# Down projections split by token half and column half; the next stage's first tiles begin on tokens 0 to 127 while the other half is normed; eight weight buffers in places; all steps placed anew

## The chip, the cores and the metric

One core of a Trainium2 chip runs the kernel. The time is device microseconds of one execution; the kernel before has a median of 1056.41 us over three runs (1062.69, 1056.41, 1053.89). One more execution was profiled. PE is TensorE (PEld its weight loads), DVE is VectorE, ACT is ScalarE, POOL is GpSimd, SP is SyncE.

## What is computed

Two transformer blocks on 256 tokens of width 1024, in fp32 (16 meta tokens are put ahead in the first block). Cut to the skeleton:

```
# first block
u = rms_norm(h, mix_pre_g);  proj = u @ w_in
y_a = hgrn2_mixer(...) @ w_hg_o;  y_b = mla_mixer(...) @ w_mla_o
h = h + rms_norm((gate_a * y_a + gate_b * y_b) @ w_out, mix_post_g)       # stage out1
u = rms_norm(h, ffn_pre_g)                                                # x2
h = h + rms_norm((silu(gt) * up) @ w_ffn_out, ffn_post_g)                 # stage ffn1, 22 tiles of 128
# second block
h = rms_norm(x, attn_pre_norm)                                            # x3
o_moba, o_nsa, o_diff, o_swa = four attentions on h @ w_in_2              # stage maps
x = x + rms_norm(mix @ w_out_2, attn_post_norm)                           # stage out2
h = rms_norm(x, ffn_pre_norm)                                             # x4
x = x + rms_norm((gelu(conv(h @ w_gate)) * (h @ w_up)) @ w_down, ffn_post_norm)   # stage ffn2, 32 tiles
```

A down projection here is any of the four products that write the 1024 columns of all tokens and are followed by a norm over those columns: out1, ffn1, out2, ffn2. The norm after it, the residual, and the next stage's own norm must be finished for a token before any matmul of the next stage can use that token.

## The kernel before

**Products.** Every large product is done with fp32r operands in two parts: a weight w is split into `wh` (rounded) and `wl = w - wh`, an activation into R parts h and l, and `three` issues three matmuls: wh with h, wh with l, wl with h. A projection tile (`gemm`) has the weights as the loaded operand and 256 tokens moving, 8 blocks x 3 = 24 matmuls of 256 columns, into one PSUM bank. A step `down` has the activations as the loaded operand and the weights moving: for a block k of 128 rows it does two token halves c (tokens 0 to 127, then 128 to 255) and in each two column halves h, 2 x 2 x 3 = 12 matmuls of 512 columns, into four banks.

**Weights.** They come in slabs of two units (a unit is 128 x 1024); three slab buffers `raw`, loaded by SP in order. A unit is made by a step `split`: ACT (or DVE) rounds it into `wh`, then DVE or POOL subtracts it into `wl`. There are four unit buffers (`NUNIT = 4`), and unit u goes into buffer u % 4, so its split waits until unit u - 4 is used. `POOL_UNITS` lists the units whose `wl` is POOL's.

**Order.** `schedule` writes one list of steps; every engine walks the whole list and does its own part of each step, strictly in this order. Where jobs are woven between projection tiles, a string of `MIX` says which comes next ("." a main step, a letter a step of that job). The list is written out by hand or by search, nothing decides at run time.

**Around a norm.** `tail` does the last blocks of a down projection (four for the 8-block ones, three for ffn1 and ffn2), first all of c = 0, then all of c = 1. Then for each c: `post` (ACT squares two column halves, DVE multiplies by the gain, then sum, variance, square root, reciprocal), `res` (DVE adds into X, two halves of 512 columns), `norm` (ACT squares X, variance, square root, reciprocal, ACT and DVE scale half of X each). Then `turn` transposes both token halves on PE, and eight steps `pre` make the h part (ACT, 256 columns) and the l part (DVE) of the next stage's operand x2, x3 or x4. Only then the next stage's first `gemm` can start. `maps` lets POOL make 12 bias tiles and lets it load two buffers `w1`, for the compression jobs `cmp_hid`.

Of the kernel before, what the change touches and what calls it, by code (L numbers as in the profile page):

```python
# [12 lines left out]
D = 1024  # L13
NM = 16
T1 = 272
HID1 = 22
HID2 = 32
LAG = 3
# [3 lines left out]
NUNIT = 4  # L22
# [116 lines left out]
class Plan:  # L139


    def __init__(self):
        self.blocks, self.at, self.slots = [], {}, []
        self.lo = lambda u: "dve"
# [7 lines left out]

    def slot(self, step, blocks, *behind):

        done = self.weights(step, blocks)
        out = [step, *behind] + [("split", u + NUNIT, self.lo(u + NUNIT), "act") for u in done]
        self.slots.append(out)
# [39 lines left out]
def down_tail(plan, name, order, order_out, mix):  # L197


    w, _, kt = DOWN[name]  # L200
    ks = order[kt - (4 if kt == 8 else LAG):]
    units = [u + NUNIT for u in plan.weights(("tail", name), [(w, 128 * k, rng(128 * j)) for k in ks for j in range(8)])]
    chain = [(kind, name, c) for c in range(2) for kind in ("post", "res", "norm")]
    order_out.append(("tail", name))
    for c in mix:
        order_out.append(chain.pop(0) if c == "." else ("split", units.pop(0)) + MAKERS[c])
    assert not chain and not units


def schedule(mixes, pool_units):  # L210
    p = Plan()
    p.lo = lambda u: "pool" if u in pool_units else "dve"
    order = [("start",)] + [("split", u, "pool" if u == 0 else "dve", "dve" if u == 0 else "act") for u in range(1)]
    order += [("turn", "x1")] + [("pre", "x1", k) for k in range(8)]
    order += [("split", u, "dve", "act") for u in range(1, NUNIT)]
    order += [("bounds",)]

    for n in range(8):
        p.tile("hf", n)
# [6 lines left out]
    order += flat(p.take())  # L226
# [24 lines left out]
    order += weave(p.take(), [metas, scan(0), scan(1), *lats, read(0) + read(1)], mixes["scan"])  # L251
# [16 lines left out]
    order += weave(p.take(), [[("o_norm",)] + [("o_scale", h) for h in range(0, 8, 2)]] + heads, mixes["latent"])  # L268

    for n in range(8):  # L270
        p.tile("yb", n)
    order += flat(p.take()) 
    for k in range(4):
        p.wide(("down", "out1", k), "w_out", k, [rng(128 * j) for j in range(8)])
    order += flat(p.take())
    down_tail(p, "out1", list(range(8)), order, mixes["out1"])

    def ffn(name, gate, up, x, nt):
        order.append(("turn", x))
        order.extend(("pre", x, k) for k in range(8))  # L280
        for i in range(nt):
# [5 lines left out]
        order.extend(flat(p.take()))  # L287
        down_tail(p, name, list(range(nt)), order, mixes[name])

    ffn("ffn1", "g1", "u1", "x2", HID1)  # L290

    order += [("maps",), ("turn", "x3")] + [("pre", "x3", k) for k in range(8)]
    o, w = IN2, "w_in_2"
    p.tile("nkc", 0, True)
    for n in range(2):
        p.tile("nq", n, True)
# [3 lines left out]
    for k in range(8):  # L300
        p.wide(("tm1", k), w, k, [rng(c) for c in (o["mv"], o["mv"] + 128, o["dv"], o["dv"] + 128)],
               *([("tm1_out",)] if k == 7 else []))
    for n in (0, 2, 1, 3):
        p.tile("d", n, True)
# [22 lines left out]
    order += weave(p.take(), jobs, mixes["maps"])  # L327
    down_tail(p, "out2", KORD2, order, mixes["out2"])
    ffn("ffn2", "g2", "u2", "x4", HID2)
    order.append(("store",))  # L330
    last = -(-len(p.blocks) // 16) * 2
    return [s for s in order if s[0] != "split" or s[1] < last], p.blocks, p.at
# [1714 lines left out]
```

## Time and profile before

| | us |
|---|---|
| three runs | 1062.69, 1056.41, 1053.89 |
| median | 1056.41 |
| profiled execution | 1064.89 |
| its span, first to last instruction | 1063.1 |
| PE busy in the span | 989.7 |
| DVE, ACT, POOL busy | 519.4, 480.3, 357.9 |
| mean granted clock of PE, 1 is full | 0.958 |

A PE that is busy is not PE at its peak: at the lower of its two clock levels it is busy for twice as long with the same matmuls. So two things are to be looked for: where PE is idle, and where its clock is low. The profiled execution took 8.5 us more than the median of the runs.

### The profile page before, as it was taken

Reading aid. Unit: us, or ns where it says so; the run is one execution under the profiler, and the core shown is the slowest. Engines: PE = TensorE matmul, PEld = TensorE weight load, DVE = VectorE, ACT = ScalarE, POOL = GpSimd, SP = SyncE. Lnnn points to the kernel's source line nnn. Section 1 sums busy time; section 2 is a strip of 40 time slices with the busy share of each in tenths; the row PEclk is TensorE's granted clock in tenths of the full one; section 3 lists DMA queues with packets and bytes.
Section 4 is the critical chain, followed back from the end, with each engine's and each line's share of the span. In section 5 each row is a group of like instructions: output and inputs, shape, how many; then the busy total and the mean of one; then the engine's idle time right before and its main releaser. Section 6 shows DMA issues by size and latency. Waiting matters only on the chain.

```text
span 1063.1 us, 16460 instructions
## 1 busy us (share of the span) xinstructions
PE 989.7 (93%) x6733; PEld 900.4 (85%) x6733; DVE 519.4 (49%) x1027; ACT 480.3 (45%) x843; POOL 357.9 (34%) x167
## 2 busy tenths in 40 slices
PE   3999999979999988999999498999979999999997
PEld 3989999967788968999999396887769999999996
DVE  5414855256424764423433625575365455465455
ACT  5424113454335355444444625366454444444443
POOL 1322221211023435244333542120064633534551
PEclk9999969999999998999999698899889999999999
DMA  7434222333133344555545343222335555554551
GB/s 270 168 131 159 80 80 104 111 123 119 40 120 140 138 158 178 176 186 186 199 166 198 118 159 105 75 90 80 119 108 190 198 174 184 199 188 173 194 174 65
DMA packets 23035, 154.80 MB, mean 146 GB/s; under 512 B 2592, under 2 KB 3104, under 8 KB 5168
## 3 DMA queue, kind: packets, MB, share of 16 engines
q1 hardware_dynamic: 22384, 151.65, 39.8%
q0 software_dynamic: 576, 2.10, 0.6%
q8 instruction: 54, 0.88, 0.3%
q14 instruction: 21, 0.17, 0.0%
HBM read 152.42 MB, written 1.05 MB: 144 GB/s over the span
## 4 chain that ended last, share of the span: by engine, by line
PE 83%; DVE 8%; ACT 5%; DMA 2%; issue 1%; SPq 0%; POOL 0%; DVEq 0%; ACTq 0%; POOLq 0%
PE pb L433 82%; ACT FA L439 3%; PE pb L436 2%; DVE FA L442 2%; DMA FA<-in_lev 1%; DVE st L442 1%; DVE wl L442 1%; DVE X L448 1%; DVE R L448 1%; ACT wh L439 1%; DVE st L445 1%; ACT R L439 1%; DMA FA<-in_w 0%; DVE FA L448 0%; SPq L469 0%
## 5 line engine op out<-in xcount | busy, mean ns | idle before, releaser
L433 PE MATMUL pb<-R,wh 128*128 128x256 f32 (+1 forms) x3056 | 570.2, 288 | 11.5 <-POOL wl L442 7.2
L442 POOL TENSOR_TENSOR wl<-raw,wh 128x1024 fp32r<-128x1024 f32 x140 | 340.5, 2438 | 654.1 <-ACT wh L439 652.0
L433 PEld LDWEIGHTS pb<-R,wh 128*128 128x128 f32 x3056 | 487.3, 194 | 22.2 <-issue 11.6
L433 PE MATMUL pb<-R,wl 128*128 128x256 f32 (+1 forms) x1528 | 437.3, 286 | 0.0
L439 ACT ACTIVATE wh<-raw 128x1024 fp32r<-128x1024 f32 x273 | 286.1, 1054 | 183.8 <-PE pb L433 183.7
L433 PEld LDWEIGHTS pb<-R,wl 128*128 128x128 f32 x1528 | 296.8, 194 | 0.0
L442 DVE TENSOR_TENSOR wl<-raw,wh 128x1024 fp32r<-128x1024 f32 x138 | 182.1, 1323 | 209.3 <-ACT wh L439 209.0
L433 PE MATMUL pb<-wh,R 128*128 128x512 f32 (+1 forms) x744 | 242.9, 393 | 1.6 <-DVE FA L457 1.0
L433 PEld LDWEIGHTS pb<-wh,R 128*128 128x128 f32 x744 | 141.2, 190 | 32.1 <-issue 2.3
L433 PE MATMUL pb<-wl,R 128*128 128x512 f32 (+1 forms) x372 | 145.2, 390 | 0.0
L439 ACT ACTIVATE FA<-pb 128x256 f32<-128x256 f32 (+7 forms) x155 | 65.7, 436 | 166.1 <-PE pb L433 147.2
L433 PE MATMUL pb<-FA 128*128 128x64 f32 (+14 forms) x696 | 111.8, 310 | 4.1 <-ACT FA L439 2.1
L433 PEld LDWEIGHTS pb<-FA 128*128 128x128 f32 (+6 forms) x696 | 88.9, 199 | 21.3 <-issue 9.9
L433 PEld LDWEIGHTS pb<-wl,R 128*128 128x128 f32 x372 | 71.1, 191 | 12.0
L436 PE MATMUL pb<-cst,FA 128*128 128x128 f32 (+4 forms) x213 | 40.4, 329 | 43.6 <-ACT FA L439 34.9
L442 DVE TENSOR_TENSOR FA<-FA,pb 128x256 f32<-128x256 f32 (+2 forms) x64 | 28.0, 437 | 94.2 <-PE pb L433 86.0
L436 PEld LDWEIGHTS pb<-cst,FA 128*128 128x128 f32 (+4 forms) x213 | 28.5, 163 | 53.4 <-ACT FA L439 31.3
L439 ACT ACTIVATE R<-FA 128x256 fp32r<-128x256 f32 (+1 forms) x66 | 28.4, 431 | 94.1 <-DVE FA L442 94.1
L442 DVE TENSOR_TENSOR R<-FA,R 128x256 fp32r<-128x256 f32 (+1 forms) x58 | 28.7, 495 | 29.0 <-ACT R L439 29.0
L439 ACT ACTIVATE FA<-FA 128x256 f32<-128x256 f32 (+7 forms) x39 | 16.0, 410 | 53.3 <-DVE FA L448 47.2
L442 DVE TENSOR_TENSOR FA<-FA 128x512 f32<-128x512 f32 (+7 forms) x68 | 38.1, 602 | 3.7 <-PE pb L433 1.8
L448 DVE SCALAR_TENSOR_TENSOR FA<-pb,sm,FA 128x255 f32<-128x255 f32 (+1 forms) x68 | 33.9, 498 | 10.4 <-ACT FA L439 8.0
(95 smaller groups left out, 408.6 us busy)
## 6 DMA issues: line engine op xcount, KB each, us to landing
raw<-in_w SPq DMA_DIRECT2D x139, 1024.0 KB, 4.8
X<-in_x SPq DMA_DIRECT2D x2, 512.0 KB, 4.4
post<-in_ffn_post SPq DMA_DIRECT2D x2, 512.0 KB, 5.6
post<-in_w POOLq DMA_DIRECT2D x2, 512.0 KB, 4.8
FA<-in_w POOLq DMA_DIRECT2D x2, 512.0 KB, 4.6
out<-X SPq DMA_DIRECT2D x4, 256.0 KB, 2.0
cst<-in_cst SPq DMA_DIRECT2D x1, 796.0 KB, 12.5
post<-in_mix_post SPq DMA_DIRECT2D x1, 512.0 KB, 3.6
```

The lines of the kernel that those rows point to most:

```text
L433: return self.real.matmul(*a, **k) if self.real else self
L436: return self.real.transpose(*a, **k) if self.real else self
L439: return self.real.activation(*a, **k) if self.real else self
L442: return self.real.tensor_tensor(*a, **k) if self.real else self
L445: return self.real.tensor_scalar(*a, **k) if self.real else self
L448: return self.real.scalar_tensor_tensor(*a, **k) if self.real else self
```

## The change

Four things are changed together.

- **Tails.** `tail` is now four steps (c, h), each all of its last four blocks for one token half and one column half, 12 matmuls of 512 columns. The last four blocks are taken everywhere (`LAG` is 4). `post` waits for each column half by itself. A partial variance is made from the first half, and one ACT instruction adds the second half and takes the root; this takes one DVE instruction out of each of the two norms.
- **Next stage by token halves.** `chain` does post, res, norm, then `turn` and two steps `op` of four blocks for one token half, then the same for the other. For x2 and x4 the first two tiles of gate and up are split: `gemm0` does the 8 matmuls of `wh` with both parts of tokens 0 to 127 (256 columns in two pieces of 128), `gemm1` later the 16 others. Their result lies in two halves of the bank, and DVE folds them (`tensor_reduce`). For x3 the value projections `tm2` and `tm1` are brought to the front, all of c = 0, then all of c = 1.
- **Buffers.** From out1's tail to the last block of x3's value projections, and again in ffn2, there are eight unit buffers; PLACE and PRIOR give each unit its buffer and the unit that it replaces. Four of them lie where upper parts of `FA` are at other times, so the first units in them wait for these (`opened`).
- **All steps placed anew.** All strings of MIX are new, and `MADE` gives every unit its makers: ACT rounds 219 units (273 before) and DVE 59 (5), DVE subtracts 176 (138) and POOL 102 (140). `maps` is moved behind the value projections; the jobs of the attentions start only after it.

The diff, cut to its core:

```
-LAG = 3
+LAG = 4
-NUNIT = 4
+NBASE = 4
+NWIDE = 8
+SPLIT_TILES = 2
...
+def chain(name, x):
+    out = []
+    for c in range(2):
+        out += [("post", name, c), ("res", name, c)]
+        if x:
+            out += [("norm", name, c), ("turn", x, c), ("op", x, c, 0), ("op", x, c, 1)]
+    return out
...
+        return [[("tail", name, c, h)] for c in range(2) for h in range(2)], units
...
+        for i in range(SPLIT_TILES):
+            for t in (gate, up):
...
+                main.append([("gemm0", t, i)])
+        main += [[("gemm1",) + s[0][1:3]] + s[1:] for s in late]
+        segs.append((down, main, [chain(down, x), refill(units, list(range(first, first + NWIDE - NBASE)))]))
...
+    main += [[s[0] + (0,)] for s in both] + [[s[0] + (1,)] + s[1:] for s in both]
+    segs.append(("ffn1", main, [chain("ffn1", "x3"), refill(units, [])]))
+    wide[0] = wide[0][0], p.next_unit()
+    fixed(("maps",))
...
-    "out1": ".p....p.pq",
+    "out1": "...............bbaaab.abaa.aaba...aaab.bb...",
...
+                elif kind == "gemm0":
...
+                        e.matmul(both, whi(u, o), OPERAND[src][:, k, :, 0:128], start=k == 0, stop=False)
+                elif kind == "gemm1":
...
+                        e.matmul(both, whi(u, o), OPERAND[src][:, k, :, 128:256], start=False, stop=False)
+                        m = e.matmul(b[:, 0:256], wlo(u, o), operand(src, k, 0), start=False, stop=k == 7)
...
+                elif kind == "op":
+                    x, c, i = a
+                    for j in range(4):
+                        k = 4 * i + j
+                        e.wait_ge(*pe.at(("turn", x, c, j)))
+                        if i:
+                            e.wait_ge(*dve.at((x, "l", j, c)))
+                        e.activation(operand(x, k, 0)[:, 128 * c:128 * c + 128], banks.of(("turn", x, c, j))[:, 128 * i:128 * i + 128],
+                                     ACT.Identity, scale=sc(PRE_GAIN[x], k)).then_inc(*act.up((x, "h", k, c)))
```

PE behind out1's last down matmuls, before: the 16 transposes of both token halves (`cst,FA`), then the first gate tile.

```order
1393 L433 MATMUL pb<-wh,R 128x512
1394 L436 MATMUL pb<-cst,FA 128x128 x16
1395 L433 MATMUL pb<-R,wh 128x256 x2
1396 L433 MATMUL pb<-R,wl 128x256
1397 L433 MATMUL pb<-R,wh 128x256 x2
```

and now:

```order
1390 L484 MATMUL pb<-wh,R 128x512
1391 L487 MATMUL pb<-cst,FA 128x128 x8
1392 L484 MATMUL pb<-R,wh 128x2x128 x32
1393 L487 MATMUL pb<-cst,FA 128x128 x8
1394 L484 MATMUL pb<-R,wh 128x2x128
1395 L484 MATMUL pb<-R,wl 128x256
```

The transposes are halved, and 32 matmuls (four `gemm0`) stand between the halves; the other 64 matmuls of these four tiles follow behind the second half (the first two rows of them are shown).

ACT in the same place, before, from the table load for the square root on (`wh<-raw` are splits, `FA,st<-pb` the squares of post, `FA,st<-X` those of norm, `R<-pb,sm` the operand):

```order
196 L439 ACT_TABLE_LOAD
197 L439 ACTIVATE st<-st 128x1
198 L439 ACTIVATE FA,st<-pb 128x512 x2
199 L439 ACTIVATE st<-st 128x1
200 L439 ACTIVATE wh<-raw 128x1024
201 L439 ACTIVATE FA,st<-X 128x512 x2
202 L439 ACTIVATE st<-st 128x1
203 L439 ACTIVATE FA<-X,st 128x512
204 L439 ACTIVATE FA,st<-pb 128x512 x2
205 L439 ACTIVATE st<-st 128x1
206 L439 ACTIVATE wh<-raw 128x1024
207 L439 ACTIVATE FA,st<-X 128x512 x2
```

and now:

```order
180 L490 ACTIVATE FA,st<-pb 128x512 x2
181 L490 ACTIVATE st<-st 128x1
182 L490 ACTIVATE FA,st<-X 128x512 x2
183 L490 ACTIVATE st<-st 128x1
184 L490 ACTIVATE FA<-X,st 128x512
185 L490 ACTIVATE wh<-raw 128x1024
186 L490 ACTIVATE R<-pb,sm 128x128 x8
187 L490 ACTIVATE FA,st<-pb 128x512 x2
188 L490 ACTIVATE st<-st 128x1
189 L490 ACTIVATE wh<-raw 128x1024
190 L490 ACTIVATE FA,st<-X 128x512 x2
191 L490 ACTIVATE st<-st 128x1
```

The eight operand instructions of c = 0 and a split now stand ahead of the first square of c = 1.

DVE in the same place, now (`FA<-pb,post` is the gain, `X<-FA,st,X` res, `R<-pb,sm,R` the l part of the operand):

```order
326 L496 TENSOR_SCALAR FA<-X,st 128x512
327 L508 CAST wh<-raw 128x1024
328 L493 TENSOR_TENSOR wl<-raw,wh 128x1024
329 L499 SCALAR_TENSOR_TENSOR R<-pb,sm,R 128x128 x8
330 L496 TENSOR_SCALAR st<-st 128x1
331 L493 TENSOR_TENSOR FA<-pb,post 128x512 x2
332 L511 RECIPROCAL st<-st 128x1
333 L499 SCALAR_TENSOR_TENSOR X<-FA,st,X 128x512 x2
334 L493 TENSOR_TENSOR wl<-raw,wh 128x1024
335 L496 TENSOR_SCALAR st<-st 128x1
336 L511 RECIPROCAL st<-st 128x1
```

A whole split of DVE stands between the scaling of X and the operand of c = 0, and a subtraction inside the norm of c = 1; before, DVE had no subtraction there.

PE behind ffn1's last down matmuls, now (before, 16 transposes and then a gate-like tile, as above):

```order
2291 L484 MATMUL pb<-wh,R 128x512
2292 L487 MATMUL pb<-cst,FA 128x128 x8
2293 L484 MATMUL pb<-wh,R 128x268
2294 L484 MATMUL pb<-wl,R 128x268
...
2325 L484 MATMUL pb<-wl,R 128x512
2326 L484 MATMUL pb<-wh,R 128x512
2327 L487 MATMUL pb<-cst,FA 128x128 x8
2328 L484 MATMUL pb<-wh,R 128x268
```

Between the transposes of the two halves stand 24 matmuls of 268 and 24 of 512 columns.

## Rows read from the trace of the kernel before

**Rows 1.** The page, part 2: busy tenths in 40 slices, and the granted clock.

```profile
PE   3999999979999988999999498999979999999997
PEclk9999969999999998999999698899889999999999
```

**Rows 2.** Busy time in windows, PE: window, busy (matmuls), clock, DMA share, GB/s.

```profile
392.00:408.00 16.00, 8.46 (x43) 0.68 0.27 99
592.00:616.00 24.00, 9.43 (x44) 0.57 0.24 88
772.00:788.00 16.00, 8.68 (x49) 0.68 0.28 98
140.00:162.00 22.00, 22.00 (x112) 0.53 0.14 48
```

**Rows 3.** The timeline behind out1's tail: start, length, engine, operation.

```profile
388.06 0.60 ACT L439 ACTIVATE FA<-pb 128x512 f32<-128x512 f32 x1 [2.86 <-PE pb L433]
...
390.39 1.42 DVE L448 SCALAR_TENSOR_TENSOR X<-FA,st,X 128x512 f32<-128x512 f32 x2
...
391.19 2.87 POOL L442 TENSOR_TENSOR wl<-raw,wh 128x1024 fp32r<-128x1024 f32 x1 [5.04 <-ACT wh L439]
...
392.60 1.47 DVE L442 TENSOR_TENSOR st<-st 128x1 f32<-128x1 f32 x1 [0.79 <-ACT FA L439]
...
393.07 0.39 PE L433 MATMUL pb<-wh,R 128*128 128x512 f32 x1
...
394.73 0.72 ACT L439 ACTIVATE FA<-X,st 128x512 f32<-128x512 f32 x1 [0.23 <-DVE st L460]
...
403.33 3.00 ACT L439 ACTIVATE R<-pb,sm 128x256 fp32r<-128x256 f32 x8
...
403.81 3.23 DVE L448 SCALAR_TENSOR_TENSOR R<-pb,sm,R 128x256 fp32r<-128x256 f32 x8 [0.97 <-ACT R L439]
404.35 0.79 PE L433 MATMUL pb<-R,wh 128*128 128x256 f32 x2
...
407.08 0.41 PE L433 MATMUL pb<-R,wh 128*128 128x256 f32 x2
...
407.44 0.40 PE L433 MATMUL pb<-R,wh 128*128 128x256 f32 x2
```

**Rows 4.** The timeline behind ffn1's tail.

```profile
591.83 5.32 POOL L442 TENSOR_TENSOR wl<-raw,wh 128x1024 fp32r<-128x1024 f32 x2 [3.61 <-ACT wh L439]
592.10 5.60 DVE L448 SCALAR_TENSOR_TENSOR X<-FA,st,X 128x512 f32<-128x512 f32 x2
...
592.36 0.39 PE L433 MATMUL pb<-wh,R 128*128 128x512 f32 x1
...
611.46 0.79 PE L433 MATMUL pb<-R,wh 128*128 128x256 f32 x2 [2.39 <-DVE R L448]
```

**Rows 5.** The timeline behind out2's tail.

```profile
772.76 0.39 PE L433 MATMUL pb<-wh,R 128*128 128x512 f32 x1
...
783.83 0.78 PE L433 MATMUL pb<-R,wh 128*128 128x256 f32 x2
```

**Rows 6.** Busy time in the window of maps: PE, PEld, DVE, ACT, POOL, clock, DMA, GB/s.

```profile
611.50:762.20 150.70, 140.23 (x906) 119.96 (x907) 75.42 (x279) 73.95 (x199) 34.47 (x26) 0.92 0.29 101
```

**Rows 7.** Groups by shape: count, busy us, mean ns of one, idle before.

```profile
L439 ACT ACT_TABLE_LOAD x16 | 20.5, 1283 | 1.0 <-PEq L2037 0.7
...
L439 ACT ACTIVATE FA<-FA,st 128x256 f32<-128x256 f32 x24 | 11.9, 496 | 0.0
...
L439 ACT ACTIVATE FA<-FA,st 128x128 f32<-128x128 f32 x24 | 9.5, 395 | 11.7 <-DVE st L445 11.7
...
L442 DVE TENSOR_TENSOR wl<-raw,wh 128x1024 fp32r<-128x1024 f32 x138 | 182.1, 1323 | 209.3 <-ACT wh L439 209.0
...
L457 DVE CAST wh<-raw 128x1024 fp32r<-128x1024 f32 x5 | 3.3, 686 | 0.5 <-PE pb L433 0.5
...
L448 DVE SCALAR_TENSOR_TENSOR FA<-FA,st 128x128 f32<-128x128 f32 x4 | 1.4, 342 | 0.0
```

More of the change, by code:

```diff
@@ L286, in ffn @@
                 p.wide(("down", name, i - LAG), DOWN[name][0], i - LAG, [rng(128 * j) for j in range(8)])
[L287 to L292, printed above, removed]
+        segs.append((None, p.take(), []))
+        return first
+    for n in range(8):
+        p.tile("yb", n)
+    for k in range(4):
+        p.wide(("down", "out1", k), "w_out", k, [rng(128 * j) for j in range(8)])
+    wide = [(ffn("ffn1", "g1", "u1", "x2", HID1, "out1", list(range(8)), p.take()), 0)]
     o, w = IN2, "w_in_2"
-    p.tile("nkc", 0, True)
-    for n in range(2):
-        p.tile("nq", n, True)
+    main, units = down_tail("ffn1", list(range(HID1)))
     for k in range(8):
@@ L326, in schedule @@
             jobs.append(plain((m, h)) + ([("join", kt + h // 2)] if h % 2 else []))
[L327 to L332, printed above, removed]
-KORD2 = [2, 3, 4, 5, 6, 7, 0, 1]
-POOL_UNITS = (5, 8, 9, 10, 14, 15, 16, 24, 25, 27, 28, 30, 31, 32, 34, 38, 39, 40, 42, 44, 47, 50, 52, 54, 60, 61, 63,
[5 rows of a table removed]
+    segs.append(("maps", p.take(), jobs))
@@ new lines, in segments @@
+    wide.append((ffn("ffn2", "g2", "u2", "x4", HID2, "out2", KORD2, []), 10 ** 6))
+    tail, units = down_tail("ffn2", list(range(HID2)))
+    segs.append(("ffn2", tail, [chain("ffn2", None)]))
+    fixed(("store",))
+    count = -(-len(p.blocks) // 16) * 2
+    last, place, prior, after = {b: -NWIDE + b for b in range(NWIDE)}, [], [], {}
+    for u in range(count):
+        n = NWIDE if any(a <= u < b for a, b in wide) else NBASE
+        b = min(range(n), key=lambda b: (last[b], b)) if u >= NBASE else u
+        place.append(b)
+        prior.append(last[b] if last[b] >= 0 else None)
+        if last[b] >= 0 and u not in early:
+            after.setdefault(last[b], []).append(u)
+        last[b] = u
@@ new lines, in named, with names @@
+    def named(s):
+        if s[0] == "free":
+            return [("split", u) for u in after.get(s[1], []) if s[1] not in behind]
+        if s[0] == "open":
+            return [("split", s[1])]
+        if s[0] == "behind":
+            return [("split", u) for u in after.get(s[1], [])]
+        return [s]
+    def names(steps):
+        return [t for s in steps for t in named(s)]
+    segs = [(key, [names(s) for s in main], [names(j) for j in jobs]) for key, main, jobs in segs]
+    return segs, p.blocks, p.at, place, prior, [a for a, _ in wide], wide[0][1]
@@ L728, in bank, with down @@
                 return b
-            def down(name, k, c, first, last):
+            def down(name, k, c, first, last, hs=(0, 1)):
                 src = DOWN[name][1]
```

389 lines of the change are left out of this document (226 added, 163 removed), and 5 rows, old and new, of the table POOL_UNITS.

## Prediction

> **What bounds the kernel now.** I read the slices first [rows 1]: PE is at nine tenths or full nearly everywhere, with a hole at the start, three marked holes in the middle (slices 15 and 16, 23, 30) and one at the end. So PE bounds, and only what fills a hole or keeps the clock up shortens the run. The middle holes are the norms behind out1, ffn1 and out2. The windows over them [rows 2] show PE busy for 8.46 of 16 us, 9.43 of 24 and 8.68 of 16, at a clock of 0.68, 0.57 and 0.68: at the lower of the two levels (1.2 of 2.4 GHz) for much of it. The timeline gives the size of each hole. The last tail matmul starts at 393.07 and lasts 0.39; the next stage's first matmul starts at 404.35 [rows 3]: 10.9 us. The 12 matmuls up to 407.08 take 2.73 us, where at full clock three take 0.36 (407.08 to 407.44), so 12 take 1.44: another 1.3 us. Behind ffn1: 592.75 to 611.46 [rows 4], 18.7 us; its clock is at the lower level to about 615.3 (estimated from the 0.57 over 24 us, which leaves 3.4 us at full clock in the window), so half of 3.8 us, 1.8 with rounding, is lost beside it, 20.5. Behind out2: 773.15 to 783.83 [rows 5], 10.7 us, and 1.0 at low clock (estimated from the 0.68 in the same way), 11.7. Sum: 12.2 + 20.5 + 11.7 = 44.4 us.
>
> Two more losses are in no hole: the clock is 0.53 over 22 us from 140 on though PE is always busy (10.3 us lost), and maps, 150.7 us long, has 10.5 us of idle PE and a clock of 0.92 (12 us) [rows 6].
>
> **A chain for one token half.** Let 0 be the end of its last tail matmul. Before, c = 0 begins at 388.06 and ACT has scaled X at 394.73 + 0.72, 7.4 us later [rows 3]. In this stand 1.3 us in which a DVE instruction of one column takes 1.47 instead of 0.15 beside POOL's subtraction that started at 391.19. Behind ffn1 it is worse: two residual additions take 5.60 beside two subtractions of POOL, against 1.42 behind out1 [rows 3, 4]. Now: the square of the first column half lies under the tail, the second takes 0.8 with its accumulator, the root and reciprocal 0.9, the residual 1.4 (rows 3: 1.42 for two), the second square of X 0.8 behind it, root and reciprocal 0.55, scaling 0.72: **5.2 us**, if POOL isn't in the way. Then the transposes (about 0.1 each, one pair is enough to begin) and `op`. An `op` instruction on 128 columns is in no row for its operands: 256 columns cost ACT 3.00 / 8 = 0.375 and DVE 0.40 apiece [rows 3], 128 cost DVE 0.34 in another form [rows 7]. I take 0.30 for a pair in step, near that row, with ends 0.20 (half of the 256-column price) and 0.40 (all of it).
>
> **out1.** PE has 24 matmuls of c = 1 to do in the meantime: 388.0 to 393.46, 5.45 us [rows 3]. ACT has a split (1.05) behind the scaling and begins `op` at 6.3. DVE has a cast and a subtraction, 0.69 + 1.25 ([rows 7]: 0.686, and 1.323 as a mean with the waits beside POOL), from 5.0 to 7.0. So the first `gemm0` matmul starts at 7.3, 1.85 after PE went idle. Its eight blocks come at 0.30 each, not at 0.12, so this tile ends at 9.5 instead of 8.3: 1.3. The other three tiles run at 0.12 x 24 = 2.9, to 12.4. The second half does not start at 5.45, since its squares stand in ACT's list behind the eight operand instructions (order of the section on the change): ACT is free at 8.6. From there two squares and their accumulators 1.6, root and reciprocal 0.9 (the gain of DVE lies between), residual 1.4, then DVE's subtraction 1.25 ahead of its part of the variance, square and root hidden or 0.3, reciprocal 0.2, scaling 0.72, transposes 0.3, first pair 0.6: 16.0. So PE is idle from 12.4 to 16.0, 3.6, and the next tile is held back by 0.5. Sum of out1: 1.85 + 1.3 + 3.6 + 0.5 = **7.3**, before 12.2. This is where the change gives less than its design: the holes are cut, not closed.
>
> **out2.** The same, with DVE's split in c = 0 placed later (operand at 8.0 instead of 7.3) and a cast instead of a subtraction in c = 1: 2.5 + 1.3 + 3.3 + 0.5 = **7.6**, before 11.7.
>
> **ffn1.** The tail has four blocks now, c = 1 gives 5.45 again. DVE's split from 5.0 to 7.0 puts the first value matmul at 7.3: 1.9 idle. `tm2` needs 0.38 a block (three of 268 columns), more than a pair's 0.30, so it runs freely, 3.0, and `tm1` 24 x 0.227 = 5.45, to 15.8. Meanwhile c = 1: ACT is free at 8.6, a split to 9.7, squares to 11.4, root and reciprocal 12.6 (DVE has a subtraction and two gains there), residual 14.0, DVE's subtraction for the last unit of tm1 15.25, root, reciprocal and scaling 16.5, operand at 17.4. PE waits 0.8 for that unit and 0.8 for the operand. Sum 1.9 + 0.8 + 0.8 = **3.5**, before 20.5. It is the largest gain, because its old hole was doubled by POOL's two instructions and 10 bias tiles and by a table load, and because 8.5 us of real work now lie in it. What hid behind those 8.5 us in maps is uncovered; see the first rival.
>
> **The end.** The first column half's square of the last chain is done before the last matmul; today two squares of 0.60 and their accumulators follow it in a row, as behind out1 [rows 3]. One goes: **0.7**.
>
> **What costs nothing.** The matmuls are as many and as long: 8 x 256 + 16 x 256 columns a split tile. Whether two pieces of 128 columns cost more than 256 in one is in no row; bounds 0 and 0.04 x 32 x 2 = 2.6 us, I take 0. Eight folds of two half banks are 0.7 each on DVE in stages where it is half idle (DVE 519 of 1063 us busy); if they weren't covered they would cost 5.4. Moving 38 subtractions from POOL to DVE (1.25 each) and 54 casts from ACT (1.05) to DVE (0.69) adds 85 us to DVE's 519, 57% of the span, and takes over 90 from POOL. Where DVE is the maker, its unit is ready sooner (0.69 + 1.25 in a row) than POOL's (1.05 + 2.4 or more, rows 3: 2.87). Four more table loads (20 in the order, 16 before) are 4 x 1.28 = 5.1 us of ACT [rows 7], and ACT waits for PE in the stages where they lie. SP's gain loads stand behind `gained` of c = 1 as before, 5 us later; three slabs are in flight by then.
>
> **The sum.** (12.2 - 7.3) + (11.7 - 7.6) + (20.5 - 3.5) + 0.7 = 26.7. Whether the clock falls in holes of 3.3 and 3.6 us is in no row; the old holes cost 1.0 and 1.3 behind them, so the bounds are 0 and 2.3, and I take off 1.1: **25.6**. In the profiled execution that makes 1064.9 - 25.6 = 1039.3. The profile took 8.5 us over the median, and its dip at 140 cost 10.3; I take this dip as a thing of single executions and set the sum against the median: 1056.4 - 25.6 = 1030.8, say **1031**. The size of `op` moves this by +4 or -2, POOL in the way of a chain by +1.3 apiece, up to four.
>
> **A rule of the notes beside the rows.** The residual additions of 2.8 us each ran beside POOL, those of 0.71 did not, while the l parts read from PSUM kept 0.40 with POOL busy from 403.50 on [rows 3, 4]. The Trainium skill, SBUF — State Buffer, section "Who interferes with whom", says that the port pair which VectorE and GpSimd share is an exclusive lock: whichever issues second is fully blocked until the other's instruction ends. By that rule, the trace agrees, and it speaks against this change too: each subtraction moved to DVE is one with two SBUF inputs that can be blocked by one of POOL's that is left. By it a chain could lose up to one POOL instruction each time; by the rows of out1 it lost 1.3. For table loads, the skill's page ScalarE: Activation LUTs, section "What ACT_TABLE_LOAD costs", adds a drain of about 1.38 us to each; with it the four would cost ACT 10.6 instead of 5.1. No row here shows a drain, and the sum is the same.
>
> **Rivals.** *Maps pays it back.* Value projections worth 20 us of PE work (all of tm1 and tm2) no longer lie between the attentions' jobs. Those are chains of ACT and DVE; now they have 51 us to hide under (14 tiles of 24 x 0.12, four `down` of 12 x 0.227), before 71. For it: even with them maps lost 22.5 us [rows 6], and behind the last projection the new list has some 50 job steps in a row. Against it: every step has been placed anew, and DVE and ACT are busy for only 75.4 and 74.0 of 150.7 us [rows 6]. If a tenth more of its 131 us is lost, that is 13 us: 1044. *The new places do more.* If the dips and waits outside the holes (22.5 in maps, 10.3 at 140) shrink by a third, 11 us: 1020. *Slower than before.* Same mechanism as the first, at another size: with the jobs begun only after tm1, PE waits for each of 20 softmaxes in turn (ACT's two exponentials 0.395 + 0.496 [rows 7], and as an estimate as much again for DVE's scores ahead of them: 1.8) and for eight joins (0.375 as ACT's operand [rows 3]), 39 us, which takes the whole gain and more: 1070. It decides from 36 us of new idle time in maps, over a quarter of it. *The change doesn't do what it says.* If `gemm0` had to wait for the whole chain (a bank or a unit that comes free only with c = 1), the holes of out1 and out2 stay: 1031 + 9 = 1040.
>
> **How the numbers follow.** Forecast 0.55, maps pays back 0.17, the new places do more 0.16, not filled 0.08, slower 0.04. The forecast's own range is 1024 to 1038; the range reaches to 1015 on the side of the second rival and 1047 on that of the first. One per cent (10.6 us, 1045.8) is about what a measurement of this kernel can tell from no change, its three runs lying 8.8 us apart: faster 0.87, same 0.09, slower 0.04.
>
> **What would show it.** Holes of about 2 + 3.6 us behind out1 and 2.5 + 3.3 behind out2, with 8 matmuls at 0.3 us spacing first; under 4 us idle behind ffn1; ACT's squares of c = 1 some 3 us after their matmuls; residual additions at 0.71. I am wrong if PE's idle time in maps grows by over 10 us, if a clock of one half follows the small holes for long, or if the ffn stages, busy without a gap before, show waits for DVE's `wl`.

## The result, and the profile after

The changed kernel took **1004.7 us** (median of four runs, 999.2 to 1007.8) beside 1057.8 for the kernel before on the same chip: ratio 0.949, 95% interval 0.943 to 0.955. Forecast were 1031 us and a gain of 26; the gain is 53 us, and the time lies 10 us below the range's low end.

The page of the kernel after, parts 1 and 2: its first line of engines, then busy tenths and granted clock in 40 slices. They answer to [rows 1].

```profile
PE 970.7 (97%) x6733; PEld 885.6 (88%) x6733; DVE 614.8 (61%) x1137; ACT 435.4 (43%) x817; POOL 272.6 (27%) x129
PE   3999999999999999999999999999999999999997
PEclk9999999999999999999999999997999999999999
```

No slice between the first and the last is under nine tenths, and the clock's rows of 6 and 8 are gone but for one 7. Span less PE's busy time makes an account that the rest of this document uses: before, 1063.1 - 989.7 = 73.4 us idle; after, 1004.4 - 970.7 = **33.7**. So 39.7 of the 58.7 us between the two profiled executions are idle time that went, and 19.0 us are the same 6733 matmuls done in less busy time, at a higher clock.

The windows of the kernel after: busy PE (matmuls), clock, DMA share, GB/s. The first three lie over the seams, as [rows 2] does before; the fourth is the same stretch of time as the last of [rows 2]; the fifth is maps, as [rows 6], but it begins 5.7 us ahead of the first projection, with the last value projection's second half, and ends 7 us inside out2's tail. The sixth is a part of maps.

```profile
366.00:386.00 20.00, 16.89 (x95) 0.91 0.41 159
566.00:590.00 24.00, 22.09 (x136) 1.00 0.28 94
718.00:736.00 18.00, 14.80 (x94) 0.91 0.48 164
140.00:162.00 22.00, 22.00 (x196) 1.00 0.27 96
585.26:716.10 130.84, 130.66 (x841) 0.92 0.32 115
675.00:695.00 20.00, 20.00 (x83) 0.57 0.15 53
```

Two of the rows are not in the forecast: 140 to 162 us has 196 matmuls where it had 112, and maps has 0.2 us of idle PE where it had 10.5. Its clock is 0.92 as before (0.91 from 590.9 to 709.0, its own bounds), most of the loss in the last window: 20 us busy at 0.57.

**The seams came as worked out.** The timeline of the kernel after behind out1's tail answers to [rows 3]:

```profile
368.55 1.41 DVE L499 SCALAR_TENSOR_TENSOR X<-FA,st,X 128x512 f32<-128x512 f32 x2
...
371.28 0.72 ACT L490 ACTIVATE FA<-X,st 128x512 f32<-128x512 f32 x1 [0.23 <-DVE st L511]
...
371.98 0.40 PE L484 MATMUL pb<-wh,R 128*128 128x512 f32 x1
372.21 1.04 PE L487 MATMUL pb<-cst,FA 128*128 128x128 f32 x8
372.86 2.21 ACT L490 ACTIVATE R<-pb,sm 128x128 fp32r<-128x128 f32 x8
...
373.55 2.15 DVE L499 SCALAR_TENSOR_TENSOR R<-pb,sm,R 128x128 fp32r<-128x128 f32 x8
374.04 4.99 PE L484 MATMUL pb<-R,wh 128*128 128x256 f32 x32 [0.79 <-ACT R L490]
...
381.31 1.30 PE L487 MATMUL pb<-cst,FA 128*128 128x128 f32 x8 [2.28 <-ACT FA L490]
...
382.65 0.55 PE L484 MATMUL pb<-R,wh 128*128 128x256 f32 x1
```

The tail of c = 0 ended at 366.9. The scaling of its half ends at 372.0, 5.1 us later (forecast 5.2), beside the tail of c = 1, which ends at 372.38 where PE used to stop. `op` on 128 columns costs 2.21 / 8 = 0.28 us on ACT and 0.27 on DVE (0.30). The first eight `gemm0` matmuls start 0.26 us apart, the others 0.118, as those of 256 columns in one piece do: the two pieces of 128 cost nothing. The first `gemm0` starts at 7.1 (7.3), the last ends at 12.1 (12.4), `gemm1` starts at 15.7 (16.0). Behind ffn1 the first value matmul comes 1.55 us after the tail, and stretches of 1.2 and 0.95 without a product follow, 3.7 in sum (3.5); 1.9 of them are idle time, the rest transposes. Behind out2 `gemm0` comes 2.2 us after the tail (2.5) and `gemm1` 3.2 after it (3.3). PE's first matmuls of each `gemm1` run at the lower clock for some 3 us, 1.3 to 1.7 us lost each.

### The profile page after: what moved, and what is told of

It is laid out like the page before. It is cut to its first block, busy times and chain, and to the rows that moved or that the text cites. A ratio compares the mean times of both kernels' runs of the same rounds, so it can differ in the third digit from the quotient of the medians.

```text
span 1004.4 us, 16498 instructions
## 1 busy us (share of the span) xinstructions
PE 970.7 (97%) x6733; PEld 885.6 (88%) x6733; DVE 614.8 (61%) x1137; ACT 435.4 (43%) x817; POOL 272.6 (27%) x129
## 4 chain that ended last, share of the span: by engine, by line
PE 91%; DVE 5%; ACT 1%; DMA 1%; issue 1%; POOL 0%; SPq 0%; DVEq 0%; ACTq 0%; POOLq 0%
PE pb L484 89%; PE pb L487 2%; DVE FA L493 2%; DMA FA<-in_lev 1%; DVE wl L493 1%; ACT FA L490 1%; DVE X L499 1%; DVE FA L514 0%; DVE R L499 0%; SPq L520 0%; ACT R L490 0%; DVE wh L508 0%; POOL wl L493 0%; DVE FA L508 0%; ACT st L490 0%
## 5 line engine op out<-in xcount | busy, mean ns | idle before, releaser
L484 PEld LDWEIGHTS pb<-R,wh 128*128 128x128 f32 x3056 | 480.5, 191 | 25.3 <-issue 15.1
L484 PE MATMUL pb<-R,wl 128*128 128x256 f32 (+1 forms) x1528 | 431.8, 284 | 0.0
L493 POOL TENSOR_TENSOR wl<-raw,wh 128x1024 fp32r<-128x1024 f32 x102 | 251.4, 2470 | 660.8 <-ACT wh L490 488.7
L493 DVE TENSOR_TENSOR wl<-raw,wh 128x1024 fp32r<-128x1024 f32 x176 | 239.0, 1371 | 113.0 <-ACT wh L490 111.7
L490 ACT ACTIVATE wh<-raw 128x1024 fp32r<-128x1024 f32 x219 | 227.2, 1053 | 116.6 <-PE pb L484 113.3
L484 PEld LDWEIGHTS pb<-wh,R 128*128 128x128 f32 x744 | 139.8, 189 | 33.7 <-DVE FA L508 2.4
L484 PEld LDWEIGHTS pb<-FA 128*128 128x128 f32 (+7 forms) x696 | 86.9, 193 | 14.8 <-issue 7.6
L508 DVE CAST wh<-raw 128x1024 fp32r<-128x1024 f32 x59 | 45.8, 778 | 23.5 <-PE pb L484 23.5
L487 PE MATMUL pb<-cst,FA 128*128 128x128 f32 (+3 forms) x213 | 34.5, 299 | 13.5 <-ACT FA L490 13.5
L487 PEld LDWEIGHTS pb<-cst,FA 128*128 128x128 f32 (+3 forms) x213 | 26.0, 151 | 19.1 <-issue 10.5
```

What stands on the lines that cost most here:

```text
L484: return self.real.matmul(*a, **k) if self.real else self
L487: return self.real.transpose(*a, **k) if self.real else self
L490: return self.real.activation(*a, **k) if self.real else self
L493: return self.real.tensor_tensor(*a, **k) if self.real else self
L508: return self.real.tensor_copy(*a, **k) if self.real else self
```

## Experiments

All are timed beside the kernel before on the same chip. A ratio to that kernel carries its interval; where two kernels of different sets of runs are compared, it is by these ratios.

**1. The kernel before, again.** No edit.

> The kernel before, unchanged, profiled once more. Its first profile shows 22.00 us of busy TensorE at a granted clock of 0.53 from 140 to 162 us, in the latent projections. Theory 1 (the stretch at half clock comes with the placement of the steps around it): the same stretch is at half clock again, within a few us, and the clock from 80 to 237 us is no higher than before, so 237 us is again about the end of the latent. Theory 2 (a thing of single executions): the clock is full there and the latent ends some 10 us earlier, near 227 us.

1065.2 us in one execution. Its windows read as those of the first profile; the last of [rows 2] is answered by

```profile
140.00:162.00 22.00, 22.00 (x113) 0.53 0.13 48
```

The half clock came back at the same place. My taking it "as a thing of single executions" fell here for the first time; experiment 7 limits this again.

**2. The new placement of scan and latent alone, in the kernel before.** (The long strings are cut to their beginnings here and below.)

```diff
-    "scan": "aa.bb.c.acbabcc.b.ba.ccb.b.c.bacb...
-    "latent": "...a.......a.a.a...a.........cbdb.decbd...
+    "scan": "a.bcabc..bcba..bbc..a.bb..ccbaa.b..a.cc...
+    "latent": "...........a..............a.da....dg.b..daa...
+MADE = <its first 82 letters>
+ORDER = [("split", s[1]) + MAKERS[MADE[s[1]]] if s[0] == "split" and s[1] < len(MADE) else s for s in ORDER]
```

> The kernel before with the changed kernel's placement of scan and latent alone: the MIX strings of these two stages and the engines of the first 82 weight steps. Nothing of the norms' split, the buffers or the later stages. Theory 1 (the changed kernel's extra gain of about 21 us up to the start of the down projections of out1 is the placement there, dips of the clock among it): 1057 - 21 = 1036 us. Rival 2 (the 10.3 us of the dip come and go by themselves; the placement gives only the idle time of TensorE there, 11 to 2 us): 1057 - 9 = 1048 us. Rival 3 (all of the gain is at the three seams and what follows them): 1057 us, no change.

**1043.1 us**, ratio 0.985 (0.981 to 0.988): 15 to 16 us gained without a touch on any norm. Idle PE fell from 73.4 to 64.5 us, busy from 989.7 to 977.3. It lies between the two expectations, 7 us above the first and 5 below the second: the 8.9 us of idle time are more than half of the gain, as the second said. Rival 3 is out.

**3. The changed kernel with the norms' overlap taken back.** Both halves of the chain now stand before the next stage's first matmul at all three seams.

```diff
-    "out1": "...............bbaaab.abaa.aaba...aaab.bb...",
-    "ffn1": "a.a.a..a...bb.a..a...b.a.....aba.aa.a...............",
+    "out1": "...............bbaaab.abaaaabaaaa....b.bb...",
+    "ffn1": "a.a.a..abbaabaabaaaa................................",
-    "out2": "..bbbaa.babb.aaa.a.aa..abaab....",
+    "out2": "..bbbaa.babb.aaaaaaabaab........",
```

> The changed kernel with the MIX strings of out1, ffn1 and out2 alone changed: both halves of the norm are finished before the next stage's first matmul, at all three seams, so that tokens 0 to 127 no longer run beside the norm of the rest. By hand from the trace of the changed kernel: the wait of TensorE at a seam grows from 7.5 to about 11.5 us at out1, from 7.6 to about 11.7 at out2, and from 3.5 to about 12 at ffn1. Theory 1 (the split is worth about what was forecast, the rest of the gain is placement elsewhere): 1004.7 + 4 + 4 + 8.5 = 1021 us. Rival (the split carries the whole of the gain of 53 us): 1040 us or more.

**1022.0 us**, ratio 0.965 (0.962 to 0.968), 17 above the changed kernel against 16.5 by hand. Idle PE is 51.3 us, 17.6 more. PE's waits by whom it waited for (total, times, longest), first this kernel, then the changed one:

```profile
PE pb L487 <- ACT FA L490: 34.3, 6, 9.4
```

```profile
PE pb L487 <- ACT FA L490: 13.5, 5, 8.9
```

The transposes of the scaled half are the one group of waits that grew by over 1 us, by 20.8 (both sums include 9 us at the kernel's start); the waits of the first products behind them shrank. So the overlap is worth what the hand walk said, and not 53 us.

**4. The changed kernel with the old placement of scan and latent**, the inverse of experiment 2 (the two MIX strings and 82 makers as before).

> The changed kernel with the old placement of scan and latent alone: the MIX strings of these two stages and the engines of the first 82 weight steps as they were before. It is the inverse of putting the new placement there into the kernel before. Theory 1 (the placement there is worth about 21 us in either kernel): 1004.7 + 21 = 1026 us, with a stretch at half clock in the latent as before. Rival 2 (only the idle time there, the dip is chance): 1004.7 + 9 = 1014 us. Rival 3 (nothing): 1005 us.

**1022.0 us**, ratio 0.965 (0.960 to 0.971): 17 us slower than the changed kernel. In its profile the 22 us from 140 on are at 0.54 again, with 114 matmuls. That profile is the slowest of four executions: they run from 1015.9 us at a mean clock of 0.986 to 1029.0 at 0.970, so the dip need not be in all of them. By the medians this placement is worth 15 to 17 us in either kernel, and it isn't borrowed from the seams.

**5 and 6. Places and engines apart**, in the kernel before: experiment 5 has only the two new strings, experiment 6 only the new engines of the 82 weight steps.

> The kernel before with the new MIX strings of scan and latent, and the old engines for every weight step. Both new together gave 1043.1 us, 14.7 below the kernel before. Theory 1 (where the narrow scan and latent steps stand among the projections decides: it takes away TensorE's waits on ScalarE and VectorE there and the stretch at half clock at 140 us): all or nearly all of it, 1043 to 1046 us, and the clock from 140 to 162 us full. Rival (the engines decide: fewer halves on GpSimd and some high halves on VectorE free ScalarE): little, 1053 to 1058 us, and the half clock stays.

> The kernel before with the new engines of the first 82 weight steps and the old MIX strings. Theory 1 (places decide): 1054 to 1058 us, half clock at 140 to 162 us as before. Rival (engines decide): 1043 to 1047 us. If both kernels show about half, 1050 us each, they add.

5: **1058.4 us**, ratio 0.998 (0.995 to 1.000). 6: **1061.1 us**, ratio 1.001 (0.998 to 1.004); its profiled execution is the longest of ten (1073.0), so only waits are read from it. Both theories fell: each edit gives at most 0.2%, the two together gave 1.5%. The timelines show why. In experiment 5, DVE and then POOL from 127 us on:

```profile
127.22 2.89 DVE L440 TENSOR_TENSOR FA<-FA 128x512 f32<-128x512 f32 x1
...
131.43 3.62 DVE L440 TENSOR_TENSOR FA<-FA 128x512 f32<-128x512 f32 x3
```

```profile
123.96 5.60 POOL L440 TENSOR_TENSOR wl<-raw,wh 128x1024 fp32r<-128x1024 f32 x2 [9.05 <-ACT wh L437]
131.42 2.88 POOL L440 TENSOR_TENSOR wl<-raw,wh 128x1024 fp32r<-128x1024 f32 x1 [1.86 <-ACT wh L437]
```

and PE behind them, then the same place in experiment 2:

```profile
135.11 3.68 PE L431 MATMUL pb<-FA 128*128 128x64 f32 x16 [2.94 <-DVE FA L440]
```

```profile
130.46 1.48 DVE L442 TENSOR_TENSOR FA<-FA 128x512 f32<-128x512 f32 x3
```

Three scan steps on DVE (two of 512 columns and one of 128; the row shows the first one's shape), two operands each in SBUF, take 1.48 us with GpSimd idle and 3.62 while GpSimd subtracts for 2.88. One of the three bears it all: the second begins 0.6 us behind GpSimd's start, takes 2.82 for 0.68 and ends 0.5 us after GpSimd. PE then waits 2.9 us, and the clock of 120 to 140 us is 0.83. Over the whole kernel experiment 5 has 70.5 us of idle PE and experiment 2 64.5: 6 of their 15 us, the rest is busy time at a lower clock. The new places put scan's steps where the old engines had GpSimd at work. In experiment 6 the waits of the old places stay (PE on ACT, 6.7 us between 80 and 370 us).

**7. The new places in maps alone**, in the kernel before, with its own engines.

```diff
-    "maps": "a......a.a..aa..a..a..a.dbbacbabdebcb.decb.dcc.bececb...
+    "maps": ".......................e.d.be.dca.eg.edbeg.gcaegdfdef.cgae.haabga.hccfcbbfd...
```

> The kernel before with the changed kernel's order of steps in maps alone: the same letters in the same order, the sixteen steps of tm2 and tm1 put back behind nkc and nq, where the kernel before has them; engines of the weight halves as before. In the profiles, TensorE's idle time in maps was 10.5 us before (140.23 busy of 150.70) and about 1 after. Theory 1 (that too is placement): 1058 - 8 to 10 = 1048 to 1050 us, with no waits on VectorE in maps over 1 us. Rival (the waits went because the weight halves are made elsewhere, or ahead in the other buffers): 1055 to 1059 us. Second rival (half clock takes the place of the waits, as the changed kernel shows for 18 us of its maps): 1053 to 1056 us, idle time gone and the mean clock in maps lower.

**1045.8 us**, ratio 0.988 (0.982 to 0.994), 12 to 13 us gained, somewhat more than theory 1's 8 to 10. In its profile the 906 matmuls of maps take 136.8 us where they took 150.7: idle PE there is 4.1 us where it was 10.5, and the clock 0.97 where it was 0.92. Waits on VectorE did not all go (1.0 and 1.1 us stay in maps), and the hole behind out2 grew by 1.0. This profile has a second finding:

```profile
140.00:162.00 22.00, 22.00 (x198) 1.00 0.27 96
```

The instructions up to here are those of the kernel before, in its order, and the clock is full. So the half clock at 140 us is neither fixed by the order nor chance alone: three of the four profiled executions with the old places and engines there have it (before, experiments 1 and 4, not this one), none of the nine with the new places and engines (experiment 14 has other engines, and 0.95 from 130 to 165 us). The executions without a profile speak for chance: the two profiled ones of the kernel before have a mean clock of 0.958, which would be 0.967 without the 20.5 us at half clock, and of 44 others beside these experiments 36 have 0.961 or more, 19 of them 0.966 to 0.969. Most of them can't have had this dip and all the others too.

**8. All of the placement that the old program can take**: experiments 2 and 7 together.

> The kernel before with the new places in scan, latent and maps and the new engines of the first 82 weight steps: everything of the new placement that the old program can take, and nothing of the norms' split or the eight buffers. If the parts add: 1057.8 - 14.7 - (what the maps alone give, 0 to 10) = 1033 to 1043 us. The rest down to 1004.7, 28 to 38 us, would then be the three seams and what goes with them, against 26.8 us worked out for them in the prediction with the end.

**1031.1 us**, ratio 0.9725 (0.967 to 0.978). The product of the two alone is 0.9846 x 0.988 = 0.9728: they add. The page says 1028.3 - 969.3 = 59.0 us idle. From here to the changed kernel the ratio is 0.949 / 0.9725 = 0.976, **25 us**, and the idle time 59.0 - 33.7 = **25.3 us**; the forecast's sum for seams and end was 25.6. Idle PE by stage, from the gaps between its matmuls (us):

| | before | experiment 8 | changed |
|---|---|---|---|
| start, to the first projection | 16.3 | 16.6 | 17.5 |
| up to out1's last tail matmul | 11.0 | 2.2 | 2.3 |
| behind out1 | 7.5 | 7.5 | 3.1 |
| behind ffn1 | 14.6 | 14.2 | 1.9 |
| maps | 10.5 | 4.1 | 0.0 |
| out2's tail and behind it | 7.3 | 8.3 | 3.4 |
| end | 6.1 | 6.1 | 5.5 |

So the step from experiment 8 is not the seams alone. They and the end give 22.2 of the 25.3 us, and maps gives 4.1 more; the start takes 0.9 back. The clock moves too: the seams have less half clock (10.2, 20.5 and 13.7 us long in experiment 8; 3.4, 0 and 3.4 in the changed kernel), and maps has more (clock 0.97 in experiment 8, 0.91 in the changed kernel's profile, 0.88 in experiment 9's), some 8 us. The step also holds the new engines behind unit 82, which experiment 13 takes back.

**9 to 12. The changed kernel again, and two tries to better it.** Experiment 10 moves three of the last out2 down projections among the narrow products of maps; 11 makes the low half of unit 0 on VectorE; 12 has both.

```diff
-...nhbhbndqlbqkciiollpkejoieojjnp.mkiqnmkpnmmqik.pp.qoqk."
+...nhbhbndqlbqkci.iollpkejoieoj.jnpmkiqnm.kpnmmqikppqoqk."
-MADE = ("qdddpdpqpdvdd...
+MADE = ("vdddpdpqpdvdd...
```

> The changed kernel once more, beside the next three on the same chip. It gave 1004.7 us (999.2 to 1007.8), and its profile shows TensorE at a granted clock of 0.57 from 675 to 695 us of 20.00 us busy, where 64-column products and transposes run without a wide gemm between them. Theory 1 (the order of steps brings the half clock there): the same stretch at 0.5 to 0.7 again. Rival (which executions have it is chance): clock 0.9 or more there, and half clock elsewhere.

> The changed kernel with three of the last four dots of MIX maps earlier: the out2 down projections of k = 2, 3 and 4 (512 columns wide, some 2.5 to 5 us each) now stand among the narrow products after moba's first score, and the last one stays. No step is added or dropped. Theory 1 (a run of narrow products without wide gemms brings the half clock; 8.6 us are lost by it from 675 to 695 us): clock 0.8 or more there, 997 to 1001 us. Rival 2 (the half clock moves to the end of maps, where now only narrow products are left, or waits on VectorE and ScalarE appear there because nothing wide covers them): 1003 to 1008 us. Rival 3 (the half clock is chance): 1005 us, same.

> The changed kernel with one letter of MADE changed: the low half of unit 0 is made on VectorE, not GpSimd. In the profile the first projection waits until 22.37 us for GpSimd (8.4 us, the longest wait but one), whose 3.22 us for that half stand behind a cast that waits for its own DMA until 17.77 us; VectorE makes such a half in 1.2 to 1.4 us and has just made its high half at 12.4 us. Theory 1 (this wait is TensorE's alone): the first product starts at about 17.3 us, when its inputs R are done, 5 us sooner, and all of it or most of it stays: 1000 to 1002 us. Rival (the next units of weights, or the DMA that is 0.73 busy there, are late next): the start is sooner but the second or third unit is waited for, 1003 to 1005 us.

> Both edits together, the low half of unit 0 on VectorE and the spread down projections of out2. If each gives what its first theory says they add, being 650 us apart: 992 to 997 us. If only one does, that one's time.

9: **1000.8 us** (995.6 to 1010.4), ratio 0.946 (0.942 to 0.951). Its profile has 0.70 from 675 to 695 us, and 0.69 from 640 to 660, where the first had 0.96. The times of its six executions follow their mean clock: 995.6 to 996.5 us at 0.989 to 0.995, 1005.1 to 1010.4 at 0.981. Idle PE is the same to 0.5 us in the two profiles, of 1006.2 and 1010.4 us; none of the faster ones was profiled.

10: **1012.9 us**, ratio 0.957 (0.954 to 0.960): 12 us slower than the changed kernel, worse than rival 2 said. The clock stayed low (0.69 from 675 to 695, 0.73 from 695 to 716), and idle PE rose from 33.7 to 39.7 us, half of the 12, with waits that the changed kernel doesn't have:

```profile
PE pb L483 <- DVE R L492: 2.4, 1, 2.4
PE pb L483 <- ACT FA L489: 2.1, 1, 2.1
PE pb L483 <- DVE FA L495: 1.3, 1, 1.3
```

A wide gemm among the narrow products did not bring the clock back, and at the end of maps it was missed as cover.

11: **993.7 us** (987.9 to 999.1), ratio 0.938 (0.935 to 0.942), 7 us faster than the changed kernel beside it: the best version here. Of experiment 9's kernel the first projection waited for GpSimd, as in the changed kernel's first profile; now the inputs are late by 0.9 us only:

```profile
14.11 0.52 PE L484 MATMUL pb<-R,wh 128*128 128x272 f32 x2 [0.89 <-DVE R L499]
```

It starts 8.3 us sooner, at 14.1 and not at the 17.3 I gave (I had waited for all eight blocks of the inputs; the first block's two parts are enough), and 7 of the 8.3 stay; PE's idle time is 25.4 us. GpSimd's cast of `lev` had stood ahead of the half that PE waited for. 12: **1004.1 us**, ratio 0.9485 (0.946 to 0.951); 1012.9 - 7.1 = 1005.8, so the two edits add, one of them the wrong way.

**13. The changed kernel with the old engines behind unit 82** (196 weight steps, 103 low halves on GpSimd for 64), all places new.

> The changed kernel with the old engines for the weight steps from unit 82 on (ffn stages, maps, all three seams); places, buffers and split as changed. GpSimd then makes 103 of these 196 low halves, not 64. Theory 1 (the new places need the new engines, as in scan and latent, since VectorE's steps with two operands in SBUF stand still while GpSimd works): TensorE waits on VectorE in maps and behind the tails again, 1008 to 1020 us. Rival (the engines matter only under scan's steps): 999 to 1005 us, the changed kernel's own time.

**1027.4 us**, ratio 0.969 (0.963 to 0.976), 21 to 24 us slower. The new engines are the second ingredient in the whole kernel. PE's largest new wait is in maps, and GpSimd's own row shows the cause:

```profile
615.81 0.80 PE L482 MATMUL pb<-R,wh 128*128 128x256 f32 x2 [5.77 <-POOL wl L491]
```

```profile
599.91 11.26 POOL L494 TENSOR_SCALAR FA<-cst 128x256 f32<-128x256 f32 x11
...
613.41 4.67 POOL L491 TENSOR_TENSOR wl<-raw,wh 128x1024 fp32r<-128x1024 f32 x2
```

Eleven bias tiles, 11.3 us of GpSimd, stand ahead of the low half that the fifth projection of maps needs (unit 164). The changed kernel makes that half on VectorE. The other part is in VectorE's steps; first this kernel, then the changed one (busy, mean ns):

```profile
L497 DVE SCALAR_TENSOR_TENSOR X<-FA,st,X 128x512 f32<-128x512 f32 x16 | 15.8, 1026 | 0.3
```

```profile
L499 DVE SCALAR_TENSOR_TENSOR X<-FA,st,X 128x512 f32<-128x512 f32 x16 | 11.3, 749 | 0.3
```

The residual additions take 4.5 us more in sum, and they lie in the chains. Idle PE is 1028.4 - 980.8 = 47.6 us, 13.9 more than in the changed kernel; the rest is busy time at a lower clock. By stage, maps has 8.5 us of the idle time and some 8 us of the clock's part, while the idle time at the three seams grows by only 3.

**14. No low half on GpSimd at all**, from experiment 11's kernel (every p of MADE a d, every q a v).

> The kernel with the first low half on VectorE (993.7 us) with no low half on GpSimd at all: 101 more on VectorE, 1.23 us each where GpSimd is out of the way. VectorE's busy time goes from 617 to at most 742 us, 75% of the span, and less by what its own steps lose beside GpSimd now. Theory 1 (GpSimd's halves cost more by standing in VectorE's way than they save): 985 to 993 us. Rival (at stretches where a unit is due every 5 us beside scan or the heads VectorE is late, and TensorE waits for wl): 998 us or more.

**1013.0 us**, ratio 0.958 (0.951 to 0.965), 19 us slower than experiment 11 by the medians. Theory 1 fell. VectorE is busy for 673.2 of 1010.4 us, 67%, less than the bound of 742 that I gave; a low half costs it 1225 ns where it cost 1371 in the changed kernel, beside GpSimd. But it is late in places: PE waits for it in five of them for `R` alone (8.3 us, longest 3.2; in experiment 11 once, 0.9). With these places 102 and 101 low halves on GpSimd are better than 141 (experiment 13) and than none.

## Why the prediction was wrong

It named the gain's direction and one of its two halves. By its own steps:

- **Right: what bounds the kernel, and the seams.** PE's three holes and the end were costed at 12.2 + 20.5 + 11.7 us before and 7.3 + 3.5 + 7.6 after, 0.7 for the end and 1.1 taken off for the clock: 25.6. The times of `gemm0` and `gemm1` came within 0.3 us, behind ffn1 PE has 3.7 us without a product (3.5), the last matmul is followed by 5.5 us where it was 6.1. By the two first traces the seams and the end have 21.6 us less idle time and, since 41 us of half clock around them became 7, busy time worth some 6 us more: 27 together. Experiment 3 undoes the overlap alone: +17 for +16.5 by hand. That experiment 8 lies just 25 us above the changed kernel is in part luck: 4 us of idle time and some 8 us of clock in maps are in it with opposite signs. With the old engines (experiment 13) the seams keep most of their gain, their idle time is only 3 us longer.
- **The step that failed: "What costs nothing".** It costed the new places of all other steps, and the move of halves from GpSimd and ScalarE to VectorE, at zero, because matmuls are as many and VectorE and ScalarE were half idle. Experiment 8 has that placement and the engines of the first 82 weight steps, nothing else, and is 28 to 29 us faster than before (ratio 0.9725). 53 = 28 + 25: this is the whole miss. Of the 28, scan and latent give 15 to 16 (experiment 2), maps 12 to 13 (experiment 7). In the profiles 14.4 us of it are idle time (73.4 to 59.0) and 20.4 are busy time; by the medians the clock's part is about half. The trace of before had shown both losses, "two more losses are in no hole", 10.3 and 22.5 us [rows 2, 6]; I read them and then gave the change nothing of them.
- **"I take this dip as a thing of single executions": too strong.** The dip at 140 us was there in three of four profiles of the old order and in none of nine with new places and engines. Experiment 7 has the old order and no dip, so it is not certain either, and most executions without a profile can't have had it beside all the other dips. Setting the sum against the median and not against the profile was right; putting the losses of clock at nothing for the new order was not.
- **The rival that came in: "the new places do more".** It had 0.16 and a third of those losses, 11 us. The mechanism was right and its size too small: of 10.5 us idle in maps 6.4 went with the new places alone (experiments 7 and 8) and all of it in the changed kernel, not a third.
- **"Maps pays it back" did not happen.** The value projections left maps, and its idle time fell to nothing. The jobs needed less cover than I gave them; that this is because they no longer wait for one another in the order in which they stood is argued, not shown. What came instead is the lower clock, some 8 us against experiment 8, where the same letters of maps and the value projections among them stand at 0.97. Only at the very end of maps is cover scarce: experiment 10 took it away and lost 12 us, 6 of them idle time. The slower rival hangs on the same mechanism and went with it.
- **Engines: right rule, wrong place.** I wrote that a chain could lose a GpSimd instruction, 1.3 us apiece, up to four. Behind the tails the residual additions indeed take 0.71 each. But the same standstill acts at scan's steps (3.62 us for 1.48, experiments 5 and 2), which were in no term, and there the engines and the places paid only together. The Trainium skill, SBUF — State Buffer, section "Who interferes with whom", calls the shared port pair an exclusive lock in which the later instruction waits for the earlier one's end. The trace agrees: of three steps the one that began behind GpSimd's subtraction of 2.88 us ended 0.5 us after it and lost 2.1. Experiment 13 gives the size for the rest of the kernel: 21 to 24 us, with a queue at GpSimd in it that is no matter of the port.
- **The clock behind small holes**: forecast 1.1 us over both, measured 1.3 to 1.7 at each, half a microsecond or more beyond the bound of 2.3 in sum. Small.
- **Small terms.** Eight folds of 0.7 us are 5.6 and not 5.4; they were covered, the ffn stages have no idle PE behind the split tiles. Of the drain that the prediction quotes beside its table loads the traces show nothing: in both profiles every load but the first begins 17 to 19 ns behind the instruction before it, and where the next one waits for nothing it begins 11 or 12 ns behind the load.

**What stays open.** Which property of the order brings the half clock. It falls while PE is busy all the time; the stretches at the low level hold many products of 64 columns, but so does 141 to 155 us in experiment 2, at full clock (48 of them and 16 more on 96 of 128 columns of the array), and interleaving wide gemms (experiment 10) did not cure it. The 20 us of busy time that the placement gave are measured as a difference of one profile each; the medians (28 us for 14.4 us idle) say that some 14 of them are lasting. Why maps runs at 0.97 in experiments 7 and 8 and at 0.91 and 0.88 in the changed kernel is open, and some 8 us hang on it. Behind unit 82 the eight buffers, the move of the value projections and the new engines were not tried apart; only the engines were taken back. Whether ScalarE's freed time matters beside VectorE's was not tried apart.

## What to carry to other kernels

When a change re-places everything, cost the losses outside the place it is named for as well: list all idle time and all time at a low clock, and for each ask what the new order does to it. Zero is a claim like any other, and here it was 28 us. The order of steps and the engine of each step are one decision: either alone gave nothing in scan and latent, both gave 1.5%, and the old engines behind unit 82 cost 21 to 24 us, two thirds of it in maps. Read the longest waits that no one has named: one letter at the kernel's start, a low half queued at GpSimd behind a cast that waits for a DMA, gave 7 us more.

## What the runs showed of the hardware

- The granted clock can stand at the lower level (0.50) for some 20 us with TensorE busy the whole time, and come back without any pause. Two executions of one order agreed to the microsecond, one of the same order up to there had none.
- Executions of one kernel spread by the clock: for the changed kernel 995.6 us at a mean of 0.994 and 1010.4 at 0.981, 15 us. Its two profiles agree in idle time to 0.5 us and differ by 4.6 us in busy time.
- Three VectorE steps with both operands in SBUF, two of 512 columns and one of 128, take 1.48 us alone and 3.62 beside a GpSimd subtraction of 2.88; the one that began behind it bears the 2.1 us. VectorE steps that read PSUM (`op`, 0.27 us) keep their pace beside GpSimd's 2.85 us subtraction from 373.03 on.
- GpSimd needs 11.26 us for eleven 128x256 bias tiles, and the low half behind them in its queue starts only at 613.41.
